# RWKV-7 scan stage: the order of a step's matmuls, the plan of the prepared work, and dummy matmuls

## The reference, cut to what matters

```python
def step(state, inp):
    r_t, w_t, k_t, v_t, kk_t, a_t = inp
    sa = jnp.einsum('bhvk,bhk->bhv', state, -kk_t)
    state = (state * w_t[:, :, None, :]
             + sa[..., None] * (kk_t * a_t)[:, :, None, :]
             + v_t[..., None] * k_t[:, :, None, :])
    return state, jnp.einsum('bhvk,bhk->bhv', state, r_t)
```

## Time and profile before

| | us |
|---|---|
| median of 3 runs (3280.31 to 3281.57) | 3280.75 |
| the profiled execution | 3283.91 |
| its span, first to last instruction | 3282.1 |
| PE busy | 2877.3 (88%) |
| VectorE (DVE) busy | 1470.7 (45%) |
| ScalarE (ACT) busy | 783.1 (24%) |
| GpSimd (POOL) busy | 105.5 (3%) |
| mean granted TensorE clock | 0.855 of full speed |

### The profile page before, as it was taken

How to read it: one execution, slowest core, us unless ns; L and a number is a source line. 1 busy time by engine, 2 the same in 40 slices (tenths; PEclk the granted TensorE clock), 3 DMA queues, 4 the chain that set the end, 5 groups by cost and what they waited for, 6 DMA issues and landing times. The chain is left out here.

```text
span 3282.1 us, 47367 instructions
## 1 busy us (share of the span) xinstructions
PE 2877.3 (88%) x18974; PEld 2652.6 (81%) x18974; DVE 1470.7 (45%) x2799; ACT 783.1 (24%) x1527; POOL 105.5 (3%) x165
## 2 busy tenths in 40 slices
PE   4589999999995999669689688786889999999995
PEld 2289999999995998367476575666789999999995
DVE  1453333333437662283573745733354433333335
ACT  1231111111104221333333333322141111111112
POOL 0000000000000000001102001010000000000000
PEclk8799999999997999665665665657889999999997
DMA  8511111111101222111010110104111111111101
GB/s 340 216 52 39 38 38 39 51 38 51 38 6 39 82 95 105 76 23 32 18 24 24 25 39 3 33 6 162 39 45 46 45 38 38 38 38 51 38 19 58
DMA packets 190798, 182.68 MB, mean 56 GB/s; under 512 B 43955, under 2 KB 163550, under 8 KB 190686
## 3 DMA queue, kind: packets, MB, share of 16 engines
q1 hardware_dynamic: 190416, 180.97, 17.1%
q10 hardware_dynamic: 270, 0.09, 0.0%
HBM read 153.05 MB, written 27.98 MB: 55 GB/s over the span
## 5 line engine op out<-in xcount | busy, mean ns | idle before, releaser
L126 PE MATMUL ff_ps<-h_hi,ff_wlo 128*128 128x384 f32 x2112 | 711.1, 337 | 12.4 <-ACT ff_s L597 7.8
L127 PE MATMUL ff_ps<-h_lo,ff_whi 128*128 128x384 f32 x2112 | 709.8, 336 | 0.0
L128 PE MATMUL ff_ps<-h_hi,ff_whi 128*128 128x384 f32 x2112 | 709.6, 336 | 0.0
L126 PEld LDWEIGHTS ff_ps<-h_hi,ff_wlo 128*128 128x128 f32 x2112 | 400.4, 190 | 13.5 <-issue 8.4
L645 DVE TENSOR_TENSOR ff_s<-ff_ps,ff_s 128x384 f32<-128x384 f32 x132 | 73.6, 558 | 752.3 <-PE ff_ps L128 750.9
L127 PEld LDWEIGHTS ff_ps<-h_lo,ff_whi 128*128 128x128 f32 x2112 | 400.2, 189 | 0.0
L128 PEld LDWEIGHTS ff_ps<-h_hi,ff_whi 128*128 128x128 f32 x2112 | 399.8, 189 | 0.0
L128 PE MATMUL ff_ps<-ff_uhi,ff_whi 128*128 128x384 f32 x1056 | 352.7, 334 | 0.0
L126 PE MATMUL ff_ps<-ff_uhi,ff_wlo 128*128 128x384 f32 x1056 | 352.7, 334 | 0.0
L127 PE MATMUL ff_ps<-ff_ulo,ff_whi 128*128 128x384 f32 x1056 | 352.7, 334 | 0.0
L597 ACT ACTIVATE ff_s<-ff_ps 128x384 f32<-128x384 f32 x132 | 65.0, 493 | 740.7 <-PE ff_ps L128 740.6
(11 more groups left out here) (269 smaller groups left out, 3773.8 us busy)
## 6 DMA issues: line engine op xcount, KB each, us to landing
md_w<-w_mod SPq DMA_DIRECT2D x9, 4096.0 KB, 25.5
ff_raw<-ffn_w_gate SPq DMA_DIRECT2D x44, 512.0 KB, 4.7
ff_raw<-ffn_w_up SPq DMA_DIRECT2D x44, 512.0 KB, 3.9
ff_raw<-ffn_w_down SPq DMA_DIRECT2D x44, 512.0 KB, 3.7
pj_raw<-w_in SPq DMA_DIRECT2D x19, 512.0 KB, 4.0
z_dram<-pj_zo SPq DMA_DIRECT2D x15, 576.0 KB, 2.9
rw_rkv<-z_dram SPq DMA_DIRECT2D x12, 576.0 KB, 5.4
x_dram<-x SPq DMA_DIRECT2D x1, 4608.0 KB, 21.8
```

The source lines that it names most:

```text
L126: pe.matmul(out, w_lo, x_hi, start=start, stop=False)
L127: pe.matmul(out, w_hi, x_lo, start=False, stop=False)
L128: return pe.matmul(out, w_hi, x_hi, start=False, stop=stop)
```

## The change

1. `rest` is split: a step's order on PE becomes S0, S1, M0, M1, Y0, Y1. `prep.pe` follows, as before.
2. `ss` becomes three items, `ss_0`, `ss_1`, `ss_2`, three of the nine matmuls each. `PREP_PLAN` says which items a step takes: `ss_j` and `a0_j` in steps 1 to 3, `w0_0` and `w0_1` in steps 4 and 5, `kk` in 6 to 8, then `w0_2`, three `a1`, three `w1` until step 15. Steps 0, 16 and 17 have none. `sqrt` and `kda0` move to step 4, behind `w0_0` on ACT; `inv` and `wide` to step 4 on DVE; `kd0` to 5, `scan0` to 10, `kda1` to 13, `kd1` to 14, `ak1` to 15; `kds` and `scan1` to 16; `rkk` alone stays in 17.
3. Each scan begins on PE with 4 dummy matmuls of 512 columns. After each step without items, so in steps 0, 16 and 17 of the first three scans and in all 18 of the last, comes one dummy matmul of 128 columns.

```diff
-def keep_clock(pe, sb, out, n):
+def keep_clock(pe, sb, out, columns, n=1):
     for _ in range(n):
-        pe.matmul(out, sb["cst"][:, C_ID:C_ID + P], sb["cst"][:, 0:512], start=True, stop=True)
+        pe.matmul(out[:, 0:columns], sb["cst"][:, C_ID:C_ID + P], sb["cst"][:, 0:columns], start=True, stop=True)
...
-def head_sums(pe, sb, ps, x):
-    for t in range(NT):
+def head_sums(pe, sb, ps, x, tiles=range(NT)):
+    for t in tiles:
...
+PREP_PLAN = {1: ("ss_0", "a0_0"), 2: ("ss_1", "a0_1"), 3: ("ss_2", "a0_2"), 4: ("w0_0", ), 5: ("w0_1", ), 6: ("kk_0", ), 7: ("kk_1", ),
+             8: ("kk_2", ), 9: ("w0_2", ), 10: ("a1_0", ), 11: ("a1_1", ), 12: ("a1_2", ), 13: ("w1_0", ), 14: ("w1_1", ), 15: ("w1_2", )}
...
-    ITEMS = ["ss"] + [f"{n}_{c}" for n in ("a0", "kk", "w0", "a1", "w1") for c in range(NC)]
+    ITEMS = [name for i in sorted(PREP_PLAN) for name in PREP_PLAN[i]]
...
-        return self.ITEMS[i - 1:i] if i else []
+        return list(PREP_PLAN.get(i, ()))
     def act_names(self, i):
         out = [x for x in self.items(i) if x[0] in "wa"]
-        return out + {2: ["sqrt"], 5: ["kda0"], 14: ["kda1"]}.get(i, [])
+        return out + {4: ["sqrt", "kda0"], 13: ["kda1"]}.get(i, [])
     def dve_names(self, i):
         out = [x for x in self.items(i) if x[0] not in "wa"]
-        return out + {3: ["inv", "wide"], 6: ["kd0"], 9: ["ak0"], 12: ["scan0"], 15: ["kd1"], 16: ["ak1"],
-                      17: ["kds", "rkk", "scan1"]}.get(i, [])
+        return out + {4: ["inv", "wide"], 5: ["kd0"], 9: ["ak0"], 10: ["scan0"], 14: ["kd1"], 15: ["ak1"], 16: ["kds", "scan1"],
+                      17: ["rkk"]}.get(i, [])
...
             if name == "sqrt":
-                self.dve_t.wait(act, "ss")
+                self.dve_t.wait(act, "ss_2")
...
-                for i, d in SD:
-                    s_part(i, d)
-                    if d:
-                        rest(i, 0)
-                        rest(i, 1)
-                        if more:
-                            prep.pe(pe, i)
+                keep_clock(pe, sb, ps[:, 7, :], 512, 4)
+                for i in range(NCH):
+                    for part in (s_part, m_part, y_part):
+                        for d in range(2):
+                            part(i, d)
+                    if more:
+                        prep.pe(pe, i)
+                    if not more or not prep.items(i):
+                        keep_clock(pe, sb, ps[:, 6, :], P)
```

More of the change, by code:

```diff
@@ L1212, in pe @@
             bank = self.ps[:, n % 2, :]
-            if name == "ss":
+            if name[0] == "s":
                 self.act_t.wait(pe, "sq")
-                last = head_sums(pe, self.sb, bank, rw.sq[:, :])
+                j = int(name[-1])
+                last = head_sums(pe, self.sb, bank, rw.sq[:, :], range(j * NC, (j + 1) * NC))
             else:
@@ L1263, in dve @@
             d = int(name[-1]) if name[-1].isdigit() else None
-            if name == "ss":
-                self.pe_t.wait(dve, "ss")
-                ins = dve.tensor_scalar(rw.inv[:, :], self.ps[:, 0, 0:2 * NT], 1e-24, None, ALU.max)
+            if name.startswith("ss"):
+                self.pe_t.wait(dve, name)
+                cols = slice(d * 2 * NC, (d + 1) * 2 * NC)
+                ins = dve.tensor_scalar(rw.inv[:, cols], self.ps[:, self.ITEMS.index(name) % 2, cols], 1e-24, None, ALU.max)
             elif name == "inv":
@@ L1596, in _ @@
                         if q == 0:
-                            keep_clock(pe, sb, out, 4)
+                            keep_clock(pe, sb, out, 512, 4)
                             dve_t.wait(pe, f"nat{d}_1")
@@ L1726, in rw_scan @@
     with Stage(nc) as st, nc.psum_tensor(fresh("c_ps"), [P, 8, 512], F32) as ps:
-        pe_t = Steps(st.sem("pe_s"), [x for i in range(NCH) for x in (f"S{i}_0", f"S{i}_1", f"M{i}_0", f"Y{i}_0", f"M{i}_1", f"Y{i}_1")] +
+        pe_t = Steps(st.sem("pe_s"), [x for i in range(NCH) for x in (f"S{i}_0", f"S{i}_1", f"M{i}_0", f"M{i}_1", f"Y{i}_0", f"Y{i}_1")] +
                      ["st0", "st1"])
@@ L1749, in s_part, with m_part @@
                     pe_t.did(f"S{i}_{d}", last)
-                def rest(i, d):
+                def m_part(i, d):
                     c = order[d][i]
@@ L1758, in rest, with y_part @@
                     pe_t.did(f"M{i}_{d}", last)
+                def y_part(i, d):
+                    c = order[d][i]
                     for h in range(2):
```

## The result

The changed kernel takes 3301.59 us (median of 4 runs, 3298.36 to 3303.53) where the kernel before takes 3280.53 in the runs beside it: a ratio of 1.0056 on record, interval 1.0044 to 1.0068 (the two medians alone give 1.0064). It is slower. The forecast was 3267.0, its range ended at 3300.

The account below looks back on a forecast made before the run. It took the scans to be bound by a nearly full PE at 1.2 GHz. First three scans -4.4, last -10.8, `rw_first` +1.5 summed to -13.7: 3270.2 us profiled, 3267.0 median; range 3205 to 3300.

Parts of the forecast that it names:

- rival B: First three scans: clock falls already in step 1, at the `sq` wait and two-column matmuls; 3285.6 us, +0.15%, chance 0.23.
- The order: Scan steps: M1 waits for DVE's S1 add, costing 0.18 us per light step at 1.2 GHz, nothing in item steps.
- The opening: Start of each scan: four 512-column dummy matmuls raise the clock and cost 5.2 us, four times.
- The stall: Step 4, first three scans: PE idle about 3.3 us behind ACT and DVE work; +1.5 us, and the clock falls.
- The chain of rows 5: Step 4's table load, `sqrt`, `inv` and `wide` in sequence, 2.82 us from load to the end of `wide`.
- The plan's other terms: Steps 5 to 17 and scan end: one item fewer, `kd0` and `kk` parted, `kds`/`scan1` moved, tail gone: -0.6 - 1.2 + 1.8 - 2.25.
- The tail: End of first three scans: last outputs to the turn's first DVE instruction shrinks from 6.7 to 4.44 us, -2.25.
- Steps with items: First three scans at 2.4 GHz: 2.7 us per item step, 3.4 with a third of the sums, 3.0 with `kk`.
- A light step at 2.4 GHz: Step without items at full clock: 2.3 us, bounds 2.2 to 2.6, from 2.36 of PE scaled by 0.54 plus 1.01.
- That light steps with their dummy hold the clock: Last scan: all 18 light steps stay at 2.4 GHz, giving -10.8 us with the opening.
- rival C: Last scan: light steps do not hold the clock either, +10.3 instead of -10.8 us; 3307, +0.8%, chance 0.15.
- `rw_first`: Once, not covered by a scan: norm chain moves behind two more items and `kk` behind `w0_1`; +1.5 us, between -1 and +2.8.

Follow-up runs that it names:

- e9_dense_old_order: `e6_dense_items` with the step order of the kernel before (first direction's output before second direction's state update); ratio 0.9888.
- e4_fill_sums: `e3_sqrt_early` plus a dummy matmul ahead of each third of the sums of squares (512 columns, then 256 twice); ratio 1.0021.
- e6_dense_items: `e3_sqrt_early` plus a dummy matmul ahead of all 18 items, 256 columns each, 512 at the first sums; ratio 0.9919.
- e1_no_dummies: The changed kernel without the opening and light-step dummy matmuls, so new order and new plan alone; ratio 1.0043.
- e3_sqrt_early: The changed kernel with `sqrt` and `kda0` one step earlier on ACT, in step 3; ratio 1.0021.
- e14_late_bare: `e13_best_of` without the dummies of the six late items (steps 10 to 15); ratio 0.9926.
- e13_best_of: `e9_dense_old_order` without the dummies of the three `kk` items; 3244.31 us, ratio 0.9888.
- e7_opening_only: Kernel before with the new order and, in the last scan alone, the opening of dummies but no 128-column dummy per step; ratio 1.0021.
- e11_dense_old_plan: `e9_dense_old_order` with the plan of the kernel before, all 18 two-column matmuls in one item; ratio 1.0016.
- e15_smaller: `e13_best_of` with about half the dummy columns: 256 at all sums, 128 at the `w0` and late items; ratio 0.9999.

## Why the prediction was wrong

**The step that failed** is "In steps 1 to 3 PE waits about 1 us for `sq` and spends 0.7 each time on two-column matmuls; I take it that they hold, less surely." They did not. The clock rose in the opening as forecast and was gone before step 2. Steps 0 to 3 took 19.40 in the first scan, as long as before, and not 13.5; over three scans that is 17.4, more than the whole forecast gain. With a dummy at every item the clock did hold, and a scan took 79 instead of 95.6 (`e9_dense_old_order`, which also has the root earlier and the old order). The fall in step 1 was rival B, with 0.23 instead of 0.38; of the forecast's own signs of being wrong, "0.50 before step 4 (B)" is the one that came. The wait for `sq`, forecast at 1 us, was only 0.44, and filling it moved the fall by a step or more but did not stop it (`e4_fill_sums`). The argument against B ("the step also has outputs and a 384-column item") did not bear: that item uses half of the array's rows, and the clock passed step 2 in all three scans only when it, too, had a dummy of 256 columns ahead of it (`e6_dense_items`).

The rest, term by term:

- *The order.* Forecast: 0.18 a light step at 1.2 GHz, nothing in the others. Measured 0.23 (3.42 against 3.19). The item steps stayed at 4.51, and the 0.5 gained in a scan with items comes from its end (8.39 instead of 9.21 from step 17's S to the turn), which was not forecast. Right in the main.
- *The opening.* 5.2 forecast. In `e1_no_dummies` the first S stands 0.2 behind the memset, in the change 6.0 to 6.4: 5.8 to 6.2.
- *The stall.* Counted to step 4, as +1.5 with PE at 2.4 GHz before it, 7.3 long in rival B. From S to S it was step 5, 7.20. The chain of rows 5 was read rightly. That it ends the clock was never put to the test in the change, since nothing was left to end; in `e3_sqrt_early`, without it, the clock fell at the same place.
- *The plan's other terms* (-0.6 - 1.2 + 1.8 - 2.25 = -2.25). From S of step 4 to the turn the first scan took 70.17 against 69.22 before; less the stall's 2.69 that is -1.7. The parting of `kd0` and `kk` brought -1.3 (forecast -1.2). The tail is what was mis-sized: from the last Y to the turn it went from 6.21 to 5.24, -1.0 and not -2.25.
- *Steps with items.* At 1.2 GHz a step with a third of the sums took 5.87, rival B had 5.8. At 2.4 GHz a bare item step was forecast at 2.7 and took 2.84 (step 10 of `e14_late_bare`), a `kk` step 3.0 and 2.87 to 3.06 (`e13_best_of`). A sum step without dummies was never seen at the full clock.
- *A light step at 2.4 GHz.* 2.3 forecast, bound 2.6, measured 2.59. The 2.36 of PE in the cold ring was scaled as a whole; the ring at the full clock goes through ACT's four copies in a row, 0.97, which the forecast did not have. 18 x 0.29 = 5.2 of the last scan's missing gain, and 1.0 more for the opening: -10.8 became -4.7, all but 0.1 of it.
- *That light steps with their dummy hold the clock*: right in the last scan of all 13 kernels that have them, and rival C false. C's mechanism is real, but for steps without the dummy (`e7_opening_only`).
- *`rw_first`*, +1.5. It did not come: from its first memset to the first matmul of `rw_chunks`, the turn included, it took 64.55 against 65.01 before, -0.5. The first scan began 1.7 later all the same; among the kernels here that begin varies from 1503.8 to 1510.7, also between those with the same plan.

Rival B's 3285.6 with the measured sizes gives + 6.1 for the last scan, + 6.8 for the others (+21.1 in all against its 3 x 4.75), and -0.5 for what lies outside the scans (+1.0 against +1.5) = 3298.0. Of the remaining 3.6, 3.4 is no term of the kernel but the choice of execution: the profiled one lay 3.2 above the median before and 0.2 below it after.

I had cited the Trainium skill (TensorE: Matmul & The Clock Gate, Why this matters for your kernels) for a gate that closes behind idle gaps only. These runs disagree. It closed in step 1 with no wait of PE longer than 0.44, and in `e11_dense_old_plan` with none longer than 0.27 between the first S and the fall; in `e7_opening_only` the waits of the steps before the fall are of 0.2 to 0.27.

The chance for slower, 0.21, held mostly a fall in the last scan. The three scans with the unsure assumption weighed more than the one with the sure one; B should have been priced with the forecast's own upper bounds as well: 2.6 for a light step is 18 x 0.3 = 5.4 more, 6.5 for the opening 4 x 1.3 = 5.2 more, and 3285.6 becomes 3296, a rival on the slower side.

## What to carry over

Dummy matmuls to raise the clock are an investment that the following steps must hold: cost it as if the clock fell at the first step that is thinner than those shown to hold, and put an opening only where every step behind it has been seen to hold (here one scan of four, then all with a dummy at each item). What held here were steps with full-array matmuls in them, not busy ones; and leave more than the least: near the edge the same kernel spreads over 40 us from one execution to the next. And a change in several parts needs each part alone: one of these was neutral at the low clock, one cost some 0.3% by itself and was worth over 1% beside a third.

## What the runs showed of the hardware

- PE's busy share does not tell whether the clock holds. It stayed down at 88% (the scans before). It fell at the end of each of these three stretches: in the change from S of step 1 to the fall (83%), in `e7_opening_only` from the first S (82%), in `e11_dense_old_plan` from the first S (93%). All three ran at the full clock (PE's columns as in the first view):

```profile
1516.87:1520.08 3.21, 2.68 (x38) 1.00 0.01 3
```

```profile
2165.58:2171.26 5.68, 4.68 (x75) 1.00 0.00 0
```

```profile
1510.23:1519.68 9.45, 8.81 (x120) 1.00 0.04 13
```

  It held through 83%, in `e9_dense_old_order`, where a 128x128 dummy of 256 columns and a 384-column item were part of the step:

```profile
1529.70:1533.64 3.94, 3.28 (x38) 1.00 0.00 0
```

  Every scan that kept the clock through its last step had in each step a matmul over the full array, a dummy or a `kk` item. That is not sufficient: the first three scans of `e15_smaller` and `e11_dense_old_plan` had one in each step too and lost it. What decides is open.
- The clock could come back in mid-scan without an opening: in step 8 of `e6_dense_items`, behind three steps' dummies and two `kk` items of full-array matmuls of 128 columns, and in step 6 of `e11_dense_old_plan`.
- A kernel close to the edge has wide times: 3271 to 3305 in `e11_dense_old_plan`, 3281 to 3300 in `e4_fill_sums`, 3256 to 3299 in `e15_smaller` (10 executions each). `e9_dense_old_order` lay within 3246.02 to 3248.74 (4 executions). The kernel before spreads over 13 us as well (3277 to 3291 in 77 executions).
